# Causal mask and row maximum of a differential attention as one VectorE instruction per softmax, and the difference written over the first exponentials

## The reference, cut to what matters

```python
def block(args):
    q_blk, i = args                                    # 128 queries
    q_pos = i * Q_BLOCK + jnp.arange(Q_BLOCK)
    sc = jnp.einsum('bhcqd,bhckd->bhcqk', q_blk, kt).astype(jnp.float32)
    causal = k_pos[None, :] <= q_pos[:, None]
    sc = jnp.where(causal, sc, -jnp.inf)
    p = jax.nn.softmax(sc, axis=-1)
    p_diff = p[:, :, 0] - lam * p[:, :, 1]
    return jnp.einsum('bhqk,bhkv->bhqv', p_diff.astype(vt.dtype), vt)
```

## Time and profile before

| | |
|---|---|
| median of 3 runs | 1771.34 us (1770.96 to 1772.16) |
| span of the profiled execution, first to last instruction | 1769.8 us |
| TensorE busy in it | 1758.9 us (99%) |
| VectorE busy in it | 1151.7 us (65%) |
| ScalarE, GpSimd busy | 739.1 us (42%), 250.7 us (14%) |
| TensorE's mean granted clock | 0.999 of full speed |

### The profile page before, as it was taken

One profiled execution on the slowest core, in us unless ns is written; L12 is line 12 of the kernel. 1 busy time (PEld: TensorE's weight loads), 2 busy tenths in 40 slices (PEclk: granted clock), 3 DMA queues, 4 the chain that ended last, 5 costly groups with the idle time before them and its releaser, 6 DMA issues.

```text
span 1769.8 us, 25045 instructions
## 1 busy us (share of the span) xinstructions
PE 1758.9 (99%) x8497; PEld 1455.0 (82%) x8497; DVE 1151.7 (65%) x1863; ACT 739.1 (42%) x1486; POOL 250.7 (14%) x557
## 2 busy tenths in 40 slices
PE   9999999999999999999999999999999999999998
PEld 7887888888888888888888888888888888888886
DVE  5328989999885774443465655776665655567676
ACT  5316666666743323443231123343333333344553
POOL 3221222222120001111100102101010000000011
PEclk9999999999999999999999999999999999999999
DMA  7421222222142222326735712223232322673443
GB/s 242 144 84 49 72 73 71 72 71 71 51 145 87 88 65 99 128 101 230 251 108 168 247 60 95 96 95 126 106 107 102 117 89 94 232 280 98 147 142 125
DMA packets 138041, 213.68 MB, mean 121 GB/s; under 512 B 7569, under 2 KB 94097, under 8 KB 136930
## 3 DMA queue, kind: packets, MB, share of 16 engines
q1 hardware_dynamic: 109200, 108.54, 19.4%
q0 software_dynamic: 28752, 104.04, 16.2%
q10 hardware_dynamic: 2, 0.00, 0.0%
HBM read 150.17 MB, written 62.39 MB: 120 GB/s over the span
## 4 chain that ended last, share of the span: by engine, by line
PE 98%; DVE 1%; issue 0%; ACT 0%; DMA 0%; POOL 0%; DVEq 0%; POOLq 0%; ACTq 0%
PE ps L2340 26%; PE ps L2672 22%; PE ps L2540 17%; PE ps L2728 12%; PE ps L2424 11%; PE ps L2440 4%; PE ps L2348 3%; PE ps L2462 2%; PE ps L2464 1%; DMA x_tile<-in_x_dram 0%; DVE pt L1559 0%; DVE ring L1559 0%; DVE neg_max L1672 0%; DVE ps L1669 0%; ACT e_t L1084 0%
## 5 line engine op out<-in xcount | busy, mean ns | idle before, releaser
L2728 PE MATMUL ps<-d_op 128*128 128x512 f32 x924 | 210.3, 389 | 0.1
L2728 PEld LDWEIGHTS ps<-d_op 128*128 128x128 f32 x924 | 173.3, 188 | 36.9 <-DVE d_op L1559 0.5
L2672 PE MATMUL ps<-s_op,t_op_T 128*128 128x512 f32 x720 | 169.9, 389 | 0.0
L2424 PE MATMUL ps<-xn,ring 128*128 128x512 f32 x672 | 167.1, 398 | 0.0
L2672 PEld LDWEIGHTS ps<-s_op,t_op_T 128*128 128x128 f32 x720 | 135.2, 188 | 28.0
L2424 PEld LDWEIGHTS ps<-xn,ring 128*128 128x128 f32 x672 | 122.5, 188 | 24.8 <-issue 0.2
L2540 PE MATMUL ps<-s_op,x_op_T 128*128 128x512 f32 x576 | 135.9, 389 | 0.0
L2540 PEld LDWEIGHTS ps<-s_op,x_op_T 128*128 128x128 f32 x576 | 108.1, 188 | 22.4
L2672 PE MATMUL ps<-hn,t_op_B 128*128 128x512 f32 x480 | 115.1, 389 | 0.0
L2672 PEld LDWEIGHTS ps<-hn,t_op_B 128*128 128x128 f32 x480 | 90.1, 188 | 18.7
L1084 ACT ACTIVATE e_t<-ps,neg_max 128x256 f32<-128x256 f32 (+7 forms) x128 | 94.1, 740 | 16.5 <-DVE neg_max L1672 15.1
(11 more groups left out here) (270 smaller groups left out, 3374.7 us busy)
## 6 DMA issues: line engine op xcount, KB each, us to landing
pair<-in_w_gate_up_dram SPq DMA_DIRECT2D x20, 1024.0 KB, 5.2
rf_pieces<-s_scratch SPq DMA_DIRECT2D x74, 256.0 KB, 2.7
x_pair<-in_w_in_dram SPq DMA_DIRECT2D x16, 1024.0 KB, 6.2
raw<-in_w_in_dram SPq DMA_DIRECT2D x26, 512.0 KB, 4.0
s_scratch<-gated_ff POOLq DMA_DIRECT2D x40, 256.0 KB, 2.5
gate_in<-gate_scratch POOLq DMA_DIRECT2D x18, 512.0 KB, 3.8
v_scratch<-v_out POOLq DMA_DIRECT2D x32, 256.0 KB, 2.6
vh<-v_scratch POOLq DMA_DIRECT2D x16, 512.0 KB, 5.3
```

The source lines that it names most:

```text
L2424: last = pe.matmul(ps[:, proj_bank(first, half), :], proj_weights(which, par, a)[:, P * k:P * (k + 1)], xn[:, b, k, HALF * half:HALF * (ha ...
L2672: last = pe.matmul(ps[:, bank, :], t_op[name][:, a, k, :], block(b, k), start=opens and (k, a, b) == (0, HH, HH), stop=(k, a, b) == (3, LL ...
L2728: last = pe.matmul(ps[:, DOWN_BANKS[product][i], :], d_op[:, g % 4, a, P * i:P * (i + 1)], d_op[:, g % 4, 2 + b, :], start=opens and (a, b ...
```

## The change

The mask becomes one 128x1024 tile, zero but for its last 128 columns, where the diagonal block lies. For step i its last w columns are added to the w scores of one softmax by one `tensor_tensor_reduce`, which writes the negated sums back over the scores in PSUM and gives their minimum, which is the negated maximum. The exponential is then taken with scale -1. There is one such instruction for each softmax, and the separate masking is gone. A semaphore increment without an instruction (`scores_seen`) follows the wait for the scores. The difference is written into the first softmax's half of `e_t`, and the transposes read it there; the mask tile takes the place of `diff`. GpSimd builds the mask in one memset of 128x1024 and one select of 128x128, after a wait that all input rows have been scaled. Ones for the spreading matmul get a tile of their own.

```diff
-        diff = at("diff", [P, 2, S], F32, RF + 16384)
+        mask = at("mask", [P, S], F32, RF + 16384)
...
-        mask = const("mask", [P, 2, P])
+        ones = const("ones", [P, P])
...
-            for c in range(2):
-                did(pool.memset(mask[:, c, :], 0.0))
-                pool.affine_select(out=mask[:, c, :], in_=mask[:, c, :], compare_op=ALU.is_ge, fill=MASKED,
-                                   base=0, pattern=[[-1, P]], channel_multiplier=1).then_inc(mask_ready, 1)
-                pool.wait_ge(mask_ready, c + 1)
+            pool.wait_ge(rows_ready, TT + 1)
+            did(pool.memset(mask[:, :], 0.0))
+            pool.affine_select(out=mask[:, S - P:S], in_=mask[:, S - P:S], compare_op=ALU.is_ge, fill=MASKED,
+                               base=0, pattern=[[-1, P]], channel_multiplier=1).then_inc(mask_ready, 1)
...
                 act.activation(e_t[:, i % 2, c, 0:w],
                                ps[:, 2 * c:2 * c + 2, :].rearrange("p a b -> p (a b)")[:, 0:w], ACT.Exp,
-                               bias=neg_max[:, i % 2, c:c + 1], accum_out=sums[:, i % 4, c:c + 1])\
+                               bias=neg_max[:, i % 2, c:c + 1], scale=-1.0, accum_out=sums[:, i % 4, c:c + 1])\
...
-                dve.scalar_tensor_tensor(diff[:, b, 0:w], e_t[:, b, 1, 0:w], d_scale[:, b:b + 1],
+                dve.scalar_tensor_tensor(e_t[:, b, 0, 0:w], e_t[:, b, 1, 0:w], d_scale[:, b:b + 1],
                                          e_t[:, b, 0, 0:w], ALU.mult, ALU.add).then_inc(diff_ready, 1)
...
-            def masked(i):
-
-                dve.wait_ge(scores_done, t.at(1))
-                block = ps[:, i // 4:i // 4 + 3:2, P * (i % 4):P * (i % 4 + 1)]
-                did(dve.tensor_tensor(block, block, mask[:, :, :], ALU.add))
-
-            def maximum(i, c):
-                dve.tensor_reduce(neg_max[:, i % 2, c:c + 1],
-                                  ps[:, 2 * c:2 * c + 2, :].rearrange("p a b -> p (a b)")[:, 0:P * (i + 1)],
-                                  AX_X, ALU.max, negate=True).then_inc(max_ready, 1)
+            def minimum(i, c):
+
+                if c == 0:
+                    dve.wait_ge(scores_done, t.at(1))
+                    dve.sem_inc(scores_seen, 1)
+                w = P * (i + 1)
+                scores = ps[:, 2 * c:2 * c + 2, :].rearrange("p a b -> p (a b)")[:, 0:w]
+                dve.tensor_tensor_reduce(out=scores, in0=scores, in1=mask[:, S - w:S], scale=-1.0, scalar=HIGHEST,
+                                         op0=ALU.add, op1=ALU.min, accum_out=neg_max[:, i % 2, c:c + 1])\
+                    .then_inc(max_ready, 1)
...
-                    masked(i)
-                    maximum(i, 0)
-                    maximum(i, 1)
+                    minimum(i, 0)
+                    minimum(i, 1)
...
-                    transpose_rows(b, diff[:, i % 2, HALF * b:HALF * b + P * blocks], blocks)
+                    transpose_rows(b, e_t[:, i % 2, 0, HALF * b:HALF * b + P * blocks], blocks)
```

More of the change, by code:

```diff
@@ L15 @@
 EPS = 1e-6
+HIGHEST = 3.0e38
 MASKED = -1e30
@@ L283, in build @@
         scores_done, max_ready, exp_done = sem("scores_done"), sem("max_ready"), sem("exp_done")
+        scores_seen = sem("scores_seen")
         diff_ready = sem("diff_ready")
@@ L646, in rstd_of @@
                                    ALU.pow).then_inc(rstd_ready, 1)
-            did(pool.memset(mask[0:1, 0, :], 1.0))
+            did(pool.memset(ones[0:1, :], 1.0))
             did(pool.memset(ident[:, :], 0.0))
@@ L1735, in _ @@
                 proj_lo_of(0, 1, half, first=True)
-            dve.wait_ge(mask_ready, 2)
+            dve.wait_ge(mask_ready, 1)
             for b in range(4):
@@ L1740, in _ @@
                 step_of(0, i, first=True)
-            with turns(dve, (HEADS - 2) // 2, {n: 4, r: 4, p: 8, t: 16, trs: 40, step: 48}):
+            with turns(dve, (HEADS - 2) // 2, {n: 4, r: 4, p: 8, t: 16, trs: 40, step: 32}):
                 for par in (1, 0):
@@ L2388, in _ @@
             for half in range(2):
-                pe.matmul(ps[:, 2 + half, :], mask[0:1, 0, :], g_pre_mix_b[0:1, HALF * half:HALF * (half + 1)],
+                pe.matmul(ps[:, 2 + half, :], ones[0:1, :], g_pre_mix_b[0:1, HALF * half:HALF * (half + 1)],
                           start=True, stop=True).then_inc(g1_landed, 1)
```

## The result

| | before | after |
|---|---|---|
| median | 1771.7 us (1770.96 to 1772.35) | 1776.84 us (1776.24 to 1778.33) |
| span of the profiled execution | 1769.8 us | 1774.5 us |
| VectorE busy in it | 1151.7 us | 1131.7 us |

The changed kernel is slower: ratio 1.0030, 95% interval 1.0021 to 1.0039, 5.1 us by the medians. The prediction had said 1770.3 us and no measurable change.

A forecast was written before the change was run, and what follows sets the result against it. TensorE's own work was taken to set a head's time, about 44.3 us. Recovered waits (first head 0.5, loop turns 0.4, last head 0.1) made -1.0 us: span 1768.8, median 1770.3 us, range 1768.8 to 1777.0.

The forecast's parts named there:

- the "issue": TensorE's waits before the transposes of the difference, no producer named: 10.1 us in 33 pieces, put down to TensorE's own work.
- The third rival: Faster: waits before the transposes are really a late difference from VectorE; 8 us given back, 1761 us, chance 0.04.
- The cost e of the combined instruction: VectorE's extra time for one combined instruction over the reduction it replaces: 0.11 us, between 0 and 0.25.
- Both slower rivals: Combined instruction has a fixed extra cost (1777 to 1781 us, chance 0.13) or runs at half speed (about 1800 us, 0.07).
- half rate: Combined instruction takes 1.04 ns more per column, so VectorE paces each head: about 1800 us, chance 0.07.
- The first rival: Fixed extra per combined instruction, from 0.25 us on, adds up over four steps a head: 1777 us at 0.35; chance 0.13.
- At the two loop turns the step in front and the step behind are each 0.24 shorter, so the 0.4 us there go: Where VectorE's loop turns, its shorter steps remove TensorE's two waits for pt: 0.4 us gained.
- Nothing in a head that TensorE paces: In heads whose time TensorE sets, VectorE's time saved, 1.9 us per head, was to gain nothing at the end.
- The first head, 0.5 us: TensorE's waits for difference and exponentials (0.6 + 0.3) follow steps VectorE paces; two shorter steps recover about 0.5 us.
- The difference in place: Difference written over the first exponentials: same operands and width, no wait added, so no cost.
- the mask on GpSimd: Building the mask: between nothing and +1.0 us of GpSimd time, hidden behind a value store that waits 3.59 us anyway.
- the scale of the exponentials: Constant scale in 128 ScalarE instructions: counted at nothing, 15 us of idle ScalarE per head covering up to 0.06 each.

## Why the prediction was wrong, point by point

- *TensorE sets the time of a head; the "issue" stands behind its own work*: right. Heads without a turn went from 44.35 and 44.31 us to 44.19 and 44.20, and the "issue" is still 10.0 us. The third rival, gaps of VectorE, is out.
- *The cost e of the combined instruction*: in the right place and somewhat high, 0.11 us predicted, 0.056 measured. VectorE's busy time per head fell by 2.5 us, not 1.9. Both slower rivals fall with it: no constant of 0.25 us, no half rate. The Trainium skill ("VectorE: DVE Perf Modes", section "Two Vector instructions with no wait between them") makes the read-out an instruction of its own; the trace agrees, with a row of 142 ns, nearly all beside the next instruction. The halved throughput of which the Trainium skill ("Vector Engine (DVE) Microarchitecture Reference", section "Points that are easy to get wrong") speaks for two sources in SBUF is not seen here for one source in PSUM, one float32 source in SBUF and an accumulator: 1248 ns for 1024 columns against 1219 of the plain reduction.
- *The first rival's time, 1777 us, came; its mechanism didn't.* The loss lies in two heads, not in eight. That 1776.84 us lies inside the stated range is luck, since the range reached so far for this rival alone. Its price for a longer step was about right (1.7 us per head by its formula, 2.16 measured with the mask twice); its condition, e above 0.25 us, isn't met.
- *"At the two loop turns the step in front and the step behind are each 0.24 shorter, so the 0.4 us there go"*: this is the step that failed. -0.4 us for the two turns was counted, the waits for pt of the earlier trace rows (the windows of the earlier trace rows would have allowed -0.8), and +6.7 came, by the windows. The prediction read the 1.53 us of the earlier trace rows as a fixed price of a turn and asked only what is absorbed of it. It didn't ask what those 1.53 us with no releaser are. They are a fetch of instructions, and how long VectorE stands there depends on where the loop lies in its instruction stream. The change moved it by 15 places, and the sum had no term for where code lies. The semaphore increments and read-outs, counted at 0 to 0.11 us as work, count as places. The sum by the windows: 6.7 - 0.5 (first head) - 4 x 0.12 (loop heads without a turn) = 5.7 us, and the attention from its first scores to those of its last step is longer by as much, 351.04 against 345.36 us. Between the spans it is 4.7; 0.7 of what is left lies ahead of the attention, whose first scores start at 126.06 us instead of 126.79, a difference that unchanged starts show as well (126.14 and 126.30 in the two written-out kernels).
- *The price of a wait there*: the prediction had no term for the clock. 1.7 of the 3.95 us that a turn costs are TensorE at the lower clock behind a wait of 2.2 us; this is the sum of rows above, no run here took the wait without the clock.
- *"Nothing in a head that TensorE paces"*: wrong by 0.12 us per head, 0.7 us in the six of the loop. By the times, TensorE stood for the keys in step 3, where its row shows it busy.
- *The first head, 0.5 us*: right, 0.53 with both written out. *The difference in place, the mask on GpSimd, the scale of the exponentials, all at nothing*: right. The first was measured alone. For the others the changed kernel with its loop written out gives the bound: it is as fast as the kernel with the mask left out, which has neither.

With the loop held, the changed kernel takes 1769.1 us: the predicted direction of the parts was sound, and was overlaid by a term that isn't in the diff's operations. Their size came close partly by luck. Of the -1.0 us predicted, -0.4 belonged to the turns, which written-out kernels don't have; the -0.6 that is left stands against -1.4 measured between the two written-out kernels, 0.7 of it in heads where the prediction had nothing. Written out, or with 8, 40 or 64 empty instructions ahead of the loop, the changed kernel takes 1768.9 to 1769.5 us, 0.14 to 0.16% under the kernel before.

## What to carry to other kernels

An idle time with no releaser at a loop turn is a quantity to explain, not a constant: see whether instruction fetches fall on it, and count how many instructions the change puts ahead of the loop and into it. Compare two versions of a kernel with the loop written out, or at a few places of the loop, before a loss is put down to an operation. And an engine that is idle 10% of a head can still have no slack in the steps that follow one another; doubling one of its operations measures that directly.

## What the runs showed of the hardware

- VectorE's loop of 317 or 333 instructions runs without any fetch at some places and with five fetches of 8 KB a turn at others; a turn then costs VectorE 1.5 to 4.3 us. At a turn without fetches the loop's first instruction starts 0.3 to 0.4 us behind the branch, with them 2.8 to 3.2.
- A wait of 2.0 to 2.4 us in TensorE's otherwise full row was followed by 3.4 us at the lower clock, twice in after and twice in the kernel before with 15 empty instructions. With the mask twice, where TensorE lacks 2.94 us in two heads in pieces of up to 0.8 us, the clock stays at 1.00.
- A float32 addition, its write-back to PSUM and a minimum over the row in one VectorE instruction cost 26 to 29 ns more than the reduction alone at 128 (312 against 286), 512 and 1024 columns, and the read-out of 142 ns runs beside the next instruction.
